# Block attention: first gates computed ahead of both values and turned by VectorE and two memory trips, the value products of heads 0 to 7 in one visit

## The reference

```python
hn = rms_norm_2(h, norm_g[1])
q, k, v, z = split(hn @ attn_w_in)            # 16 heads of 64 each
q, k = norm(q) * q_norm_g, norm(k) * k_norm_g
s = q @ k.T - slope[head] * distance          # -inf for later keys
out = softmax(s) @ v
h = h + (out * silu(z)) @ attn_w_out
```

## Time and profile before

| | us |
|---|---|
| runs of the kernel before | 885.16, 884.72, 885.12 (median 885.12) |
| the profiled execution | 885.33 |
| its span (first to last instruction) | 883.5 |
| TensorE busy with matmuls in it | 879.2 (100%) |
| VectorE busy | 673.1 (76%) |
| ScalarE busy | 498.3 (56%) |
| GpSimd busy | 86.9 (10%) |

### The profile page before, as it was taken

The page is one execution under the profiler, slowest core; times in us unless marked ns, Lnnn a source line. Parts: engine busy times, 40 slices in busy tenths (PEclk is TensorE's granted clock), DMA queues, the critical chain, the costliest instruction groups (busy, mean ns, idle before and its releaser), DMA issues.

```text
span 883.5 us, 11988 instructions
## 1 busy us (share of the span) xinstructions
PE 879.2 (100%) x4272; PEld 728.3 (82%) x4272; DVE 673.1 (76%) x1031; ACT 498.3 (56%) x812; POOL 86.9 (10%) x104
## 2 busy tenths in 40 slices
PE   9999999999999999999999999999999999999998
PEld 8988888888888888778888888888888888887777
DVE  6997689766647699997787666654879987689963
ACT  6666464444445576788564444434666444588750
POOL 1002010000000403111010000000110000134410
PEclk9999999999999999999999999999999999999999
DMA  9754668676667667433387666765687774757831
GB/s 339 262 186 163 218 247 311 245 253 244 247 221 242 229 213 247 145 114 119 108 281 265 244 244 244 264 225 196 236 300 260 240 249 160 293 168 247 278 119 48
DMA packets 86083, 196.87 MB, mean 223 GB/s; under 512 B 7492, under 2 KB 38596, under 8 KB 86024
## 3 DMA queue, kind: packets, MB, share of 16 engines
q1 hardware_dynamic: 83544, 189.15, 62.0%
q0 software_dynamic: 2048, 6.29, 2.1%
q10 hardware_dynamic: 432, 0.66, 0.2%
HBM read 176.41 MB, written 19.66 MB: 222 GB/s over the span
## 4 chain that ended last, share of the span: by engine, by line
PE 92%; DVE 6%; ACT 1%; issue 1%; DVEq 0%; ACTq 0%
PE bank L1861 82%; PE bank L1899 3%; DVE wlo L1131 2%; PE bank L2178 1%; PE bank L2277 1%; DVE df_tok L1553 1%; DVE df_m L1549 1%; PE bank L1914 1%; DVE df_stat L1573 1%; PE bank L2258 1%; DVE df_ss L1525 1%; PE bank L2152 0%; PE bank L1960 0%; PE bank L2244 0%; PE bank L2067 0%
## 5 line engine op out<-in xcount | busy, mean ns | idle before, releaser
L1131 DVE TENSOR_TENSOR wlo<-raw,whi 128x1024 fp32r<-128x1024 f32 x295 | 346.4, 1212 | 32.7 <-ACT whi L737 32.4
L737 ACT ACTIVATE whi<-raw 128x1024 fp32r<-128x1024 f32 x295 | 301.5, 1059 | 116.1 <-PE bank L1861 98.1
L1861 PE MATMUL bank<-whi,x_hi 128*128 128x512 f32 x560 | 152.4, 394 | 0.0
L1861 PE MATMUL bank<-wlo,x_hi 128*128 128x512 f32 x560 | 149.8, 389 | 0.0
L1861 PE MATMUL bank<-whi,x_lo 128*128 128x512 f32 x560 | 149.8, 389 | 0.0
L1861 PEld LDWEIGHTS bank<-wlo,x_hi 128*128 128x128 f32 x560 | 105.1, 188 | 22.2
L1861 PEld LDWEIGHTS bank<-whi,x_lo 128*128 128x128 f32 x560 | 105.1, 188 | 21.9
L1861 PEld LDWEIGHTS bank<-whi,x_hi 128*128 128x128 f32 x560 | 103.6, 188 | 22.4 <-issue 1.2
L1861 PE MATMUL bank<-whi,y_hi 128*128 128x512 f32 x396 | 107.6, 394 | 0.0
L1861 PE MATMUL bank<-whi,y_lo 128*128 128x512 f32 x396 | 106.1, 390 | 0.0
L1861 PE MATMUL bank<-wlo,y_hi 128*128 128x512 f32 x396 | 106.0, 389 | 0.0
(11 more groups left out here) (263 smaller groups left out, 890.7 us busy)
## 6 DMA issues: line engine op xcount, KB each, us to landing
raw<-stream_dram SPq DMA_DIRECT2D x295, 512.0 KB, 4.7
ffn_blocks<-ffn_blk SPq DMA_DIRECT2D x22, 256.0 KB, 2.2
ffn_land<-ffn_blocks SPq DMA_DIRECT2D x22, 256.0 KB, 4.4
residual_blocks<-h_blk SPq DMA_DIRECT2D x20, 256.0 KB, 2.0
h_land<-residual_blocks SPq DMA_DIRECT2D x20, 256.0 KB, 2.9
cv_blocks<-cv_blk SPq DMA_DIRECT2D x7, 256.0 KB, 3.9
cv_land<-cv_blocks SPq DMA_DIRECT2D x7, 256.0 KB, 3.4
h_blocks<-h_blk SPq DMA_DIRECT2D x3, 512.0 KB, 2.9
```

The lines of the kernel that those rows point to most:

```text
L737: A(whi[:, u % RING, :], raw[:, u % SLOTS, :], ACT.Copy).then_inc(sem("w_hi"), 1)
L1131: V.tensor_tensor(wlo[:, u % SLOTS, :], raw[:, u % SLOTS, :], whi[:, u % RING, :].bitcast(F32), ALU.subtract).then_inc(sem("w_lo"), 1)
L1861: last = T.matmul(bank[pair + t][:, :], lhs[a][:, kt, t * P:(t + 1) * P], w[:, place(w, u), kk * NW:(kk + 1) * NW], start=part != 1 and k ...
```

## The change

- The gates' first tile moves to place 4, ahead of both value tiles, which take places 5 and 6 (`MB_STREAM`, `MB_V`, `MB_Z`).
- On TensorE `zT` 0 and 1 are gone; `av` 0 to 3 stand in one visit ahead of unit 26 (before: 0 and 1 ahead of 22, 2 and 3 ahead of 27); `scores` 6 and 7 stand ahead of unit 23 (before 24).
- VectorE turns the first gates itself: `zn` 0 and 1 and a new step `zblk` 0 and 1 (four transposes of 128x256 in 32x32 blocks) stand ahead of `max` 6. GpSimd's queue sends the blocks to memory and back (`mb_z_out`, `mb_z_in`), into the room of `mb_sq`. `y` 0 and 1 (`mb_y_early`) multiply with them from SBUF.
- The blocks of heads 12 and 13 are sent before heads 8 to 11 are fetched.
- ScalarE's order of tiles follows: gates (Silu) now between `exp` 7 and `exp` 8.
- Three semaphores are counted in one (`dve_const`).

```diff
-MB_QK, MB_V, MB_Z = (0, 1, 2, 3), (4, 6), (5, 7)
-MB_STREAM = (0, 1, 3, 4, 2, 6, 5, 7)
+MB_QK, MB_V, MB_Z = (0, 1, 2, 3), (5, 6), (4, 7)
+MB_STREAM = (0, 1, 3, 4, 6, 2, 5, 7)
...
-        (16, "scores", 3), (19, "qkT", 3), (20, "scores", 4), (20, "scores", 5), (22, "av", 0), (22, "av", 1),
-        (24, "scores", 6), (24, "scores", 7), (27, "av", 2), (27, "av", 3), (29, "zT", 0), (29, "zT", 1),
...
+        (16, "scores", 3), (19, "qkT", 3), (20, "scores", 4), (20, "scores", 5), (23, "scores", 6), (23, "scores", 7),
+        (26, "av", 0), (26, "av", 1), (26, "av", 2), (26, "av", 3), (32, "av", 4), (32, "av", 5), (32, "av", 6),
...
+        zblk = [moT[:, 4 + 2 * n:6 + 2 * n, :].rearrange("p k s -> p (k s)") for n in range(2)]
+        zland = msq65[:, :, :, :].rearrange("p t a e -> p (t a e)")[:, 0:2 * NW].rearrange("p (g n) -> p g n", g=2)
...
+            def mb_z_out(g):
+
+                pool.wait_ge(sem("mb_zblk"), g + 1)
+                nc.gpsimd.dma_start(z_dram[g], zblk[g]).then_inc(sem("mb_z_out"), 16)
+
+            def mb_z_in():
+
+                pool.wait_ge(sem("mb_z_out"), 2 * 16)
+                for g in range(2):
+                    nc.gpsimd.dma_start(zland[:, g, :].rearrange("p (i w) -> p i w", i=P // B),
+                                        z_dram[g].rearrange("q n -> (q n)").rearrange("(i p w) -> p i w", i=P // B, p=P))\
+                        .then_inc(sem("mb_z_land"), 16)
...
             mb_out(8)
             mb_out(9)
+            mb_z_out(0)
+            mb_z_out(1)
+            mb_z_in()
             mb_out(10)
             mb_out(11)
+            mb_out(12)
+            mb_out(13)
             mb_in(8)
             mb_in(9)
             mb_in(10)
             mb_in(11)
-            mb_out(12)
-            mb_out(13)
...
+            def mb_zblk(g):
+
+                dve.wait_ge(sem("mb_zn"), g + 1)
+                for t in range(TT):
+                    last = V.transpose(zblk[g].rearrange("p (f k t b) -> p t f k b", f=P // B, k=2, t=TT)[:, t],
+                                       mz[:, t, g * SEQ:(g + 1) * SEQ].rearrange("p (k b f) -> p f k b", b=B, f=P // B))
+                last.then_inc(sem("mb_zblk"), 1)
```

More of the change, by code:

```diff
@@ L187 @@
         (10, "qkT", 0), (11, "qkT", 1), (12, "scores", 0), (12, "scores", 1), (15, "qkT", 2), (16, "scores", 2),
-        (16, "scores", 3), (19, "qkT", 3), (20, "scores", 4), (20, "scores", 5), (22, "av", 0), (22, "av", 1),
-        (24, "scores", 6), (24, "scores", 7), (27, "av", 2), (27, "av", 3), (29, "zT", 0), (29, "zT", 1),
-        (32, "av", 4), (32, "av", 5), (32, "av", 6), (32, "av", 7), (34, "zT", 2), (34, "zT", 3),),
+        (16, "scores", 3), (19, "qkT", 3), (20, "scores", 4), (20, "scores", 5), (23, "scores", 6), (23, "scores", 7),
+        (26, "av", 0), (26, "av", 1), (26, "av", 2), (26, "av", 3), (32, "av", 4), (32, "av", 5), (32, "av", 6),
+        (32, "av", 7), (34, "zT", 2), (34, "zT", 3),),
     "act": (
@@ L193 @@
         (13, "exp", 2), (13, "exp", 3), (14, "qkT", 2), (16, "tile", 3), (16, "exp", 4), (16, "exp", 5),
-        (16, "exp", 6), (18, "exp", 7), (18, "qkT", 3), (20, "tile", 4), (20, "exp", 8), (20, "exp", 9),
-        (20, "exp", 10), (20, "exp", 11), (22, "oT", 0), (24, "exp", 12), (24, "exp", 13), (25, "exp", 14),
-        (25, "exp", 15), (26, "tile", 5), (27, "oT", 1), (28, "tile", 6), (29, "yhi", 0), (30, "yhi", 1),
+        (16, "exp", 6), (18, "exp", 7), (18, "qkT", 3), (19, "tile", 4), (20, "exp", 8), (20, "exp", 9),
+        (20, "exp", 10), (20, "exp", 11), (22, "exp", 12), (22, "exp", 13), (23, "tile", 5), (23, "exp", 14),
+        (23, "exp", 15), (26, "oT", 0), (26, "oT", 1), (28, "tile", 6), (29, "yhi", 0), (30, "yhi", 1),
         (32, "tile", 7), (32, "oT", 2), (32, "oT", 3), (34, "yhi", 2), (35, "yhi", 3),),
@@ L201 @@
         (15, "max", 2), (15, "sums", 3), (15, "max", 3), (17, "unit", 3), (17, "blk", 4), (17, "blk", 5),
[L202 to L205, removed]
+        (18, "blk", 6), (18, "blk", 7), (18, "max", 4), (19, "max", 5), (19, "zn", 0), (19, "zn", 1), (20, "blk", 8),
+        (20, "blk", 9), (20, "zblk", 0), (20, "zblk", 1), (22, "max", 6), (22, "blk", 10), (23, "blk", 11),
+        (23, "max", 7), (24, "blk", 12), (24, "blk", 13), (25, "blk", 14), (25, "blk", 15), (28, "y", 0),
+        (28, "y", 1), (29, "ylo", 0), (30, "ylo", 1), (32, "zn", 2), (32, "zn", 3), (33, "y", 2), (34, "ylo", 2),
+        (34, "y", 3), (35, "ylo", 3),),
 }
@@ L428, in build @@
         mb_dram = nc.dram_tensor("mb_blocks", (MB_H, P, 3 * P), F32, kind="Internal").ap()
+        z_dram = nc.dram_tensor("gate_blocks", (2, P, NW), F32, kind="Internal").ap()
         s_dram = nc.dram_tensor("residual_blocks", (len(PIECES), P, NW), F32, kind="Internal").ap()
@@ L1510, in _ @@
             HD2 = DF_HD // 2
-            V.memset(dsq65[:, :, :, DF_HD:DF_HD + 1], DF_HD * EPS).then_inc(sem("df_eps"), 1)
+            V.memset(dsq65[:, :, :, DF_HD:DF_HD + 1], DF_HD * EPS).then_inc(sem("dve_const"), 1)
             lrow = rows[:, R_LAM:R_LAM + 4 * DF_HD].rearrange("p (a b e) -> p a b e", a=2, b=2)
@@ L1607, in _ @@
             dve.wait_ge(sem("df_rot"), 4)
-            dve.wait_ge(sem("df_eps"), 1)
+            dve.wait_ge(sem("dve_const"), 1)
             for u, step, arg in df_order("dve"):
@@ L1631, in _ @@
             ffn(1, Y)
-            V.memset(cu[:, :, 0:CONV_K - 1], 0.0).then_inc(sem("cv_pad"), 1)
+            V.memset(cu[:, :, 0:CONV_K - 1], 0.0).then_inc(sem("dve_const"), 1)
             def conv_product(t):
@@ L1687, in conv_parts @@
                                 Y[0][:, bass.ds(blk, 1), :].bitcast(F32), ALU.subtract).then_inc(sem("cv_lhs"), 1)
-            dve.wait_ge(sem("cv_pad"), 1)
+            dve.wait_ge(sem("dve_const"), 2)
             conv_product(CV_IN)
@@ L1710, in _ @@
             second_lo(7, X, "mb", END[MB_IN])
-            V.memset(msq65[:, :, :, MB_HD:MB_HD + 1], MB_HD * EPS).then_inc(sem("mb_eps"), 1)
+            V.memset(msq65[:, :, :, MB_HD:MB_HD + 1], MB_HD * EPS).then_inc(sem("dve_const"), 1)
             V.tensor_copy(mgain[:, 0:1], cols[:, C_QG:C_QG + 1])
             V.tensor_scalar(mgain[:, 1:2], cols[:, C_KG:C_KG + 1], MB_HD ** 0.5, None, ALU.mult).then_inc(sem("mb_gain"), 1)
-            dve.wait_ge(sem("mb_eps"), 1)
+            dve.wait_ge(sem("dve_const"), 3)
             def mb_max(i):
@@ L1751, in mb_zn, with mb_y_early @@
                                 ALU.mult).then_inc(sem("mb_zn"), 1)
+            def mb_zblk(g):
[4 more added lines that the diff above has]
+                last.then_inc(sem("mb_zblk"), 1)
+            def mb_y_early(g):
+                dve.wait_ge(sem("mb_z_land"), 2 * 16)
+                dve.wait_ge(sem("mb_oT"), g + 1)
+                for k in range(2):
+                    o = moT[:, 2 * g + k, :].rearrange("p (t i b) -> p t i b", t=TT, b=B)
+                    V.tensor_tensor(o, o, zland[:, g, :].rearrange("p (i k t b) -> p k t i b", i=P // B, k=2, t=TT)[:, k],
+                                    ALU.mult).then_inc(sem("mb_y"), 1)
             def mb_y(g):
-                dve.wait_ge(sem("mb_zT_filled"), g + 1)
+                if g < 2:
+                    mb_y_early(g)
+                    return
+                dve.wait_ge(sem("mb_zT_filled"), g - 1)
                 dve.wait_ge(sem("mb_oT"), g + 1)
@@ L1782, in _ @@
                     mb_y(arg)
+                elif step == "zblk":
+                    mb_zblk(arg)
                 elif step == "ylo":
```

## The result

| | before | changed |
|---|---|---|
| median, us | 884.99 (884.72 to 885.16, 7 runs) | 888.16 (886.58 to 890.06, 7 runs) |
| profiled execution, us | 885.33, span 883.5 | 888.25, span 886.4 |
| ratio | | 1.0033, 95% interval 1.0023 to 1.0043 |

A forecast was written before the change was run, and what follows sets the result against it. The prediction took TensorE's queue, busy in 100% of the span, as the bound: 885.33 - 1.28 saved + 3.0 of wait = 887.05, less 0.2 for the median gives 886.8 us, range 883.7 to 889.1.

The forecast's parts named there:

- What TensorE saves: TensorE's queue in block attention: 0.91 for the dropped `zT` visit plus 0.37 for joined `av`, together 1.28 us shorter.
- term for `av` 0 to 3: TensorE in block attention: four `av` in one visit instead of two and two save 0.37 us.
- The wait of 3.0: Large visit ahead of unit 26: TensorE waits from 834.55 to 837.5 for the chain through ScalarE and VectorE, 3.0 us.
- two blockers together: Ahead of unit 26: VectorE's additions of `max` 7 end at 837.5, ScalarE's evacuation of the value tile at 837.3.
- What is hidden: Block attention: gates' trips and late fetches of heads 8 to 15 land before TensorE needs them, adding no time.
- The cover of 2.5 us: Second large visit: heads 8 to 15 land by 856.5, the fourth pair asks at 859; 2.5 us of room.
- The rule of the drain: ScalarE's table switches: a skill page adds a 1.38 us drain each, giving 889.6; the prediction kept 1.28 per load.
- Table loads that hide: ScalarE between `exp` 7 and `exp` 8: loads overlap its waits, TensorE's wait is 0.7, time 884.5; chance 0.22.
- The clock falls in the wait: TensorE after the 3 us pause: the array runs slow for a time, giving 889 to 890.5 us; chance 0.17.
- the likeliest case: Whole kernel: the wait costs only its length, giving 886.8 us, own range 886.3 to 887.5; chance 0.55.
- What spoke against it: Against a clock fall: the page's clock digit never falls, even across the start, and 1.5 us of waits left no trace.
- Half of that is lost, 2.2 to 3.7: Clock fall's size after the pause: half of a slow state of 4.4 to 7.5 us, taken from the execution's start.

The follow-up runs named there:

- experiment 6: Experiment 1's kernel with heads 8 to 11 fetched ahead of `mb_z_in`, and heads 14 and 15 sent right behind 12 and 13: 884.01 us, ratio 0.9988.
- experiment 5: Kernel before the change, with only the `av` of heads 0 to 7 put in one visit ahead of unit 27: 884.84 us, ratio 0.9998.
- experiment 1: Changed kernel with `max` 6 and 7 ahead of `zblk`, and heads 10 and 11 sent ahead of the gates' trips: 884.49 us, ratio 0.9992.
- experiment 2: Changed kernel with the gate tile at place 4 evacuated by Copy instead of Silu, so without its table loads (output not valid): 884.46 us.
- experiment 3: Changed kernel with one `wlo` moved from ahead of `max` 6 to behind the additions of `max` 7: 885.51 us.
- experiment 7: Changed kernel with two more block transposes on VectorE ahead of pair 6: 889.45 us, ratio 1.0053.
- experiment 4: Changed kernel with four more block transposes on VectorE ahead of `max` 6, each gate transpose issued twice: 890.69 us, ratio 1.0063.

## Why the prediction was right and wrong

- **The direction and the range held, in part by luck**: slower, 888.16 in 883.7 to 889.1. The number was 1.4 too low. The mechanism that it was made of, a shorter queue and one wait, gives 886.8, and the five runs of the changed kernel whose clock stays at 1.0 lie there (886.58 to 886.87). That alone is 0.2% slower, at the edge of what can be told. What makes the result clearly slower is the fall of the clock, to which the prediction gave 0.17 and a time of 889 to 890.5; one fall came to 888.2 to 888.6, below that case.
- **What TensorE saves, 1.28**: measured 1.16 in the profile of experiment 6 and 1.12 in its median, where no wait covers it. Right to 0.15, and 0.1 of that is the second visit there. Its term for `av` 0 to 3, 0.37, is 0.37 in the trace of experiment 5.
- **The wait of 3.0** from 834.55 to 837.5: measured 2.97, from 834.15 to 837.12. Each link stood where it was put: both loads 1.28, `zblk` 2.12 for 2.2, `max` 6 at 831.38 for 831.8 (TensorE comes to the stage 0.47 earlier), two blockers together. Experiments 1, 2 and 3 take away one link each: the wait goes to 0, 0.6 and 1.9, where none, 0.7 and 1.8 were expected. Experiments 7 and 4 add to one: it goes to 4.0 and 5.0, where 4.0 and 5.1 were expected.
- **What is hidden**: the trips of the gates and the fetches of heads 8 to 15 cost nothing in the changed kernel. The cover of 2.5 us was real but is thin: experiment 1, which sends the first visit off earlier and the gates later, lost it by 0.8.
- **The rule of the drain**: no row agrees with it. After the load at 814.45 the next instruction starts 0.02 behind its end, after the one at 817.98 0.01. Keeping 1.28 was right, and experiment 2 confirms it from the other side: two loads are worth 2.4. The Trainium skill, "ScalarE: Activation LUTs", section "What ACT_TABLE_LOAD costs", adds a drain of 1.38 to each load; by an estimate from that page two switches would be worth 5.3, and the trace does not agree.
- **Table loads that hide** (0.22) did not come about: the first stood behind the wait for unit 19, as the order showed.
- **The step that failed is "The clock falls in the wait", chance 0.17.** The sum went by a wait that costs its own length and nothing else, and the likeliest case was that. In 7 of 12 runs the clock fell, so the median contains a fall. What spoke against it was no evidence. Waits of 1.5 us in all say nothing of one of 3.0. The clock digit of the page cannot show 3.4 us at half rate in a slice of 22: the mean is 0.92, still a 9. And that it is 9 "even across the start" says nothing of the start, because the granted clock reads 1.00 there in short stretches too (columns as above), while four transposes take 1.06 instead of 0.60:

```profile
3.00:6.00 3.00, 3.00 (x11) 2.60 (x10) 0.07 (x2) 1.11 (x3) 0.00 (x0) 1.00 1.01 336
```

So a clock of 1.00 in the profile is not enough by itself; the lengths of equal rows have to agree with it. The fall behind the wait is in both: granted clock 0.50, and rows of 2.83 and 1.85 against 1.52 and 1.47. I did not go on to ask what the time would be if this pause were the first of its length to count.
- **Its size was also off.** "Half of that is lost, 2.2 to 3.7" was worked out from 4.4 to 7.5 us of slow rows at the start of the execution. Measured are 3.4 us at half rate, 1.6 to 1.7 lost, and twice that in two runs. In hindsight, 886.8 + 1.6 = 888.4 would have met the median, which was 888.16, to 0.2. The slow start was no measure for it: in the profile of the changed kernel it was over by 4.47.
- The Trainium skill, "TensorE: Matmul & The Clock Gate", section "Part 1: The HAM clock gate", has the rule that an idle array goes to half rate. The stretches above agree, 0.50 behind a pause of 2.97, though five of twelve such runs kept 1.0. It was named in the prediction and given too little weight beside an argument from the page's digit.

## What to carry to other kernels

On a kernel whose TensorE is busy throughout, a wait of TensorE can have two prices: its length and a fall of the clock behind it. Here waits of up to 1.9 us cost only their length, 3.0 cost 1.6 or more on top in over half of the runs, 4.0 and 5.0 in all, so shortening the wait by one `wlo` (1.1 us) gained 2.7. Before adding work to an engine that is half idle, look for what it does between two links of a chain: two table loads of 1.28 were worth 2.4 of the 3.0 of this wait; and where a new item is put into one queue, put what is due first ahead of it in every queue that both pass.

## What the hardware showed that was not expected

- A pause of one length can cost nothing or 1.6 or 3.2 us beside its length, in executions of one program: at 3.0 us 5, 5 and 2 of 12 runs. The larger loss, with a mean clock of 0.996, was seen in times and mean clocks alone, since no profiled execution had one; at 4.0 us it was 2.6 in two of five runs, at 5.0 us 2.4 in one of four, so it is not always twice the loss of one fall. Why it comes stays open.
- The fall does not come with the pause but near its end: from 0.1 before TensorE starts again (changed kernel) to 1.2 after it (experiment 7), and it lasted 3.4 us in each of the four profiled executions that have one, with TensorE busy in it.
- Even after 5.0 us of waiting (experiment 4) the granted clock was 1.00 until 839.3, when TensorE started again (839.32), and the loss in the profiled execution was no larger than after 3.0, 1.7 against 1.6.
- The granted clock of the profile reads 1.00 from the first microsecond on, though TensorE's rows at the start are slow (1.06 instead of 0.60 for four transposes), and the end of that slow start differs by some us between executions: it was over by 4.47 in the changed kernel's profile, and after 6.4 in the one before.
